# Block sums of the down projection's weights made by accumulating DMAs in DRAM, ten tiles in seven products, six raw slots

## The reference, cut to what matters

```python
def conv_gated_ffn(h, w_up, conv_w, conv_b, w_down):
    u = h @ w_up
    up = jnp.pad(u, ((0, 0), (CONV_W - 1, 0), (0, 0)))
    c = conv_b + sum(up[:, j:j + S] * conv_w[j] for j in range(CONV_W))
    gate, val = c[..., :D_FF], c[..., D_FF:]
    return (jax.nn.silu(gate) * val) @ w_down
...
    x = x + mixed @ w_o[l]
    h = rms_norm(x, norm_ffn[l])
    x = x + conv_gated_ffn(h, w_up[l], conv_w[l], conv_b[l], w_down[l])
return rms_norm(x, norm_final)
```

## Time and profile before

| | |
|---|---|
| time, median of 3 runs | 1064.83 us (1064.59 to 1065.46) |
| profiled execution | 1064.66 us, its span 1062.9 us |
| PE busy, share of the span | 1053.1 us, 99% |
| DVE | 803.6 us, 76% |
| ACT | 614.6 us, 58% |
| POOL | 9.6 us, 1% |
| moved by DMA | 201.65 MB, mean 190 GB/s |
| PE's granted clock | 0.999 |

### The profile page before, as it was taken

How to read it: one execution, slowest core, us unless ns; L and a number is a source line. 1 busy time by engine, 2 the same in 40 slices (tenths; PEclk the granted TensorE clock), 3 DMA queues, 4 the chain that set the end, 5 groups by cost and what they waited for, 6 DMA issues and landing times.

```text
span 1062.9 us, 17535 instructions
## 1 busy us (share of the span) xinstructions
PE 1053.1 (99%) x5963; PEld 908.0 (85%) x5963; DVE 803.6 (76%) x1193; ACT 614.6 (58%) x946; POOL 9.6 (1%) x30
## 2 busy tenths in 40 slices
PE   9999999999999999999999999999999999999997
PEld 8888888888888888888888888888888888888885
DVE  5677677776555787777877778777777989988886
ACT  6956475746455655555555555555555655545553
POOL 1000000000000000000000000000000000000000
PEclk9999999999999999999999999999999999999999
DMA  9575656554556566655666556665566666665663
GB/s 295 175 236 160 182 172 178 161 177 139 184 173 194 167 203 190 194 179 180 201 193 194 180 178 199 195 194 181 175 201 195 212 200 204 199 218 177 216 207 129
DMA packets 171330, 201.65 MB, mean 190 GB/s; under 512 B 8580, under 2 KB 138340, under 8 KB 171168
## 3 DMA queue, kind: packets, MB, share of 16 engines
q1 hardware_dynamic: 170576, 199.59, 60.1%
q0 software_dynamic: 400, 1.27, 0.4%
q10 hardware_dynamic: 320, 0.34, 0.1%
HBM read 199.06 MB, written 2.11 MB: 189 GB/s over the span
## 4 chain that ended last, share of the span: by engine, by line
PE 98%; DMA 1%; DVE 0%; SPq 0%; ACT 0%; issue 0%; DVEq 0%
PE tr_ps L1507 15%; PE pj L1507 15%; PE pj L1259 9%; PE pj L1509 8%; PE tr_ps L1509 8%; PE pj L1247 5%; PE pj L1248 5%; PE pj L1249 5%; PE pj L1261 5%; PE sc_ps L1247 5%; PE sc_ps L1248 5%; PE sc_ps L1249 5%; PE pj L1274 3%; PE pj L1276 1%; PE tr_ps L1248 1%; PE tr_ps L1247 1%
## 5 line engine op out<-in xcount | busy, mean ns | idle before, releaser
L798 DVE TENSOR_TENSOR split<-raw,split 128x1024 fp32r<-128x1024 f32 x282 | 340.9, 1223 | 146.4 <-ACT split L486 140.8
L486 ACT ACTIVATE split<-raw 128x1024 fp32r<-128x1024 f32 x276 | 287.6, 1057 | 105.5 <-PE pj L1509 33.0
L1507 PE MATMUL tr_ps<-act_split,split 128*128 128x512 f32 x704 | 245.5, 392 | 0.0
L1507 PE MATMUL pj<-act_split,split 128*128 128x512 f32 x704 | 245.0, 391 | 0.0
L1509 PE MATMUL pj<-act_split,split 128*128 128x256 f32 x704 | 197.1, 280 | 0.0
L1509 PE MATMUL tr_ps<-act_split,split 128*128 128x256 f32 x704 | 197.1, 280 | 0.0
L1507 PEld LDWEIGHTS pj<-act_split,split 128*128 128x128 f32 x704 | 131.6, 187 | 28.9
L1507 PEld LDWEIGHTS tr_ps<-act_split,split 128*128 128x128 f32 x704 | 131.7, 187 | 28.8
L1259 PE MATMUL pj<-act_split,split 128*128 128x512 f32 x416 | 147.8, 399 | 0.0
L1509 PEld LDWEIGHTS tr_ps<-act_split,split 128*128 128x128 f32 x704 | 133.1, 189 | 0.0
L1509 PEld LDWEIGHTS pj<-act_split,split 128*128 128x128 f32 x704 | 133.1, 189 | 0.0
(11 more groups left out here) (244 smaller groups left out, 1498.1 us busy)
## 6 DMA issues: line engine op xcount, KB each, us to landing
raw<-w_up SPq DMA_DIRECT2D x176, 512.0 KB, 4.3
raw<-w_down SPq DMA_DIRECT2D x88, 512.0 KB, 4.4
raw<-w_in SPq DMA_DIRECT2D x72, 512.0 KB, 3.8
raw<-w_o SPq DMA_DIRECT2D x32, 512.0 KB, 4.3
nat<-x SPq DMA_DIRECT2D x8, 256.0 KB, 6.6
key_bias<-nft_dram SPq DMA_DIRECT2D x4, 512.0 KB, 5.1
result<-nat SPq DMA_DIRECT2D x7, 256.0 KB, 3.1
gfin<-norm_final POOLq DMA_DIRECT2D x1, 1024.0 KB, 5.0
```

What stands on the lines that cost most here:

```text
L486: act.activation(hi[:, slot, 0:TILE], raw[:, slot, 0:TILE], ACT.Copy).then_inc(hi_done, 1)
L798: dve.tensor_tensor(lo[:, slot, 0:n], raw[:, slot, 0:n], hi[:, slot, 0:n].bitcast(F32), ALU.subtract).then_inc(lo_done, 1)
L1507: pe.matmul(up_banks[v][b].rearrange("p (a n) -> p a n", a=2), wh[:, c, b * P:(b + 1) * P], act_split[:, :, k, :], start=k == 0, stop=Fals ...
```

## The change

Ten tiles, kt 4 to 13, are done in seven products instead of seven tiles, and SUMS_AFTER sets them closer together. The sums of weight blocks are no longer added by DVE: from the third tile of w_o until 24 tiles before the end of the up projection Pool issues, for each of the 20 pairs of kt and group, two copies of 512 KB from w_down into two new DRAM tensors (t13_dram, t42_dram) and then accumulating DMAs of 256 KB within DRAM: T1 and T3, then T2 onto W22, then T4 onto W21. Six DMAs a sum, spread over four rounds, each step paced by PE's tile count (pace) and waiting for the DMAs of the round before; tsum_s counts finished sums. In the down projection SP loads all parts: part 0 whole, part 1 its half (W22, 256 KB), parts 2 and 3 from the DRAM sums. Two more slots, raw_4 and raw_5, stand where t13 and t24 stood, so loads go up to six tiles ahead. The order of the products in parts 2 and 3 changes with the layout of t42_dram. S1 is kept in the place of A21 in g_hi and g_lo, the other three in s_hi and s_lo with 384 columns. The buffers whole and sums of combine become two sets. combine takes four tiles instead of five. The squares and gains of the first two column blocks move from the start of group 1 to behind its last sums tile, and gfin is loaded once group 0 is combined.

```diff
-SUM_KT = (2, 4, 6, 8, 10, 12, 14)
+SUM_KT = tuple(range(4, 14))
 PLAIN_KT = tuple(kt for kt in range(DOWN_TILES) if kt not in SUM_KT)
-SUMS_AFTER = ((5, 9, 12, 15, 18, 22, 25), (5, 8, 11, 14, 16, 19, 21))
+SUMS_AFTER = ((5, 6, 7, 8, 11, 12, 14, 15, 18, 19), (4, 5, 6, 7, 9, 10, 12, 13, 14, 15))
+EXTRA = 2
+COMBINE = {0: (0,), 1: (1, 2), 2: (3,), 3: (4,)}
 A11, A21, A12, A22 = (0, 0), (0, 1), (1, 0), (1, 1)
-S3, S1, S2, S4 = range(4)
+S2, S4, S3, S1 = range(4)
...
-def loaded(d):
-
-    return d[1] == "plain" or d[2] < 2
-
-
 def sums_index(t):
 
     return sum(1 for d in DOWN[:t] if d[1] == "sums" and d[2] == 0)
 
 
-LOADS = [t for t, d in enumerate(DOWN) if loaded(d)]
-
-
 def raw_slot(t):
 
-    return LOADS.index(t) % RING
+    return t % RING if t < 2 * RING else (t - RING) % (RING + EXTRA)
+
+
+def raw_before(t):
+
+    return [s for s in range(t) if raw_slot(s) == raw_slot(t)]
 
 
 def slot_loads(t):
 
-    return T_DOWN // RING * 16 + (32 if raw_slot(t) % 2 == 0 else 0) + 16 * (LOADS.index(t) // RING + 1)
+    slot = raw_slot(t)
+    return (T_DOWN // RING * 16 + (32 if slot % 2 == 0 else 0) if slot < RING else 0) + 16 * (len(raw_before(t)) + 1)
+
+
+TSUMS = 2 * len(SUM_KT)
+TSUM_LAGS = 5
+TSUM_FIRST, TSUM_LAST = T_WO + 2, T_DOWN - 24
...
-        t13 = sb("t13", [P, TILE])
+        raw_4 = sb("raw_4", [P, TILE])
         assert sbuf.cursor <= top
+        sbuf.cursor = region_end
+        duo_0 = sb("duo_0", [P, MT, 512])
         sbuf.cursor = top
-        t24 = sb("t24", [P, TILE])
+        raw_5 = sb("raw_5", [P, TILE])
         assert sbuf.cursor <= nc.sbuf_usable_end
         sbuf.cursor = act_at
-        s_hi = sb("s_hi", [P, len(SUM_KT), 512], R32)
-        s_lo = sb("s_lo", [P, len(SUM_KT), 512], R32)
-        duo = sb("duo", [P, MT, 512])
-        whole, sums = duo[:, 0], duo[:, 1]
+        s_hi = sb("s_hi", [P, len(SUM_KT), 384], R32)
+        s_lo = sb("s_lo", [P, len(SUM_KT), 384], R32)
         assert sbuf.cursor <= act_end
         sbuf.cursor = act_at
         z_gain = sb("z_gain", [P, MT, 512])
+        duo_1 = sb("duo_1", [P, MT, 512])
+        wholes, sums_of = (duo_0[:, 0], duo_1[:, 0]), (duo_0[:, 1], duo_1[:, 1])
+        whole, sums = wholes[0], sums_of[0]
...
-        d_w = [sem(f"d_w{i}") for i in range(RING)]
+        d_w = [sem(f"d_w{i}") for i in range(RING + EXTRA)]
+        t_copy, t_first, t_second, t_third = [[sem(f"{n}{i}") for i in range(2)] for n in (
+            "t_copy", "t_first", "t_second", "t_third")]
+        tsum_s = sem("tsum_s")
...
+        t13_dram = nc.dram_tensor("t13_dram", (TSUMS, P, TILE), F32).ap()
+        t42_dram = nc.dram_tensor("t42_dram", (TSUMS, P, TILE), F32).ap()
...
-        def down_source(t):
-
-            if loaded(DOWN[t]):
-                return raw[:, raw_slot(t)]
-            return t13 if DOWN[t][2] == 2 else t24
+        def down_raw(t):
+
+            return raw[:, raw_slot(t)] if raw_slot(t) < RING else (raw_4, raw_5)[raw_slot(t) - RING]
...
-            for i, t in enumerate(LOADS):
-                g, kind, part, kt = DOWN[t]
-                sp.wait_ge(lo_done, T_DOWN + (LOADS[i - RING] + 1 if i >= RING else i - (RING - 1)))
-                sp.dma_start(wide(raw, raw_slot(t)),
-                             wdn[kt][:, :, (2 * g + part) * 512:(2 * g + part + 1) * 512]).then_inc(d_w[raw_slot(t)], 16)
+            for t, (g, kind, part, kt) in enumerate(DOWN):
+                if t < RING:
+                    sp.wait_ge(lo_done, T_DOWN + t - (RING - 1))
+                elif raw_before(t):
+                    sp.wait_ge(lo_done, T_DOWN + raw_before(t)[-1] + 1)
+                else:
+                    sp.wait_ge(glo_s, UP_STEPS)
+                dst = down_raw(t)[:, 0:TILE]
+                if kind == "plain" or part == 0:
+                    sp.dma_start(dst.rearrange("p (c n) -> p c n", c=2),
+                                 wdn[kt][:, :, (2 * g + part) * 512:(2 * g + part + 1) * 512]).then_inc(d_w[raw_slot(t)], 16)
+                elif part == 1:
+                    sp.dma_start(dst[:, 512:TILE], wdn[kt][:, 1, (2 * g + 1) * 512:(2 * g + 2) * 512]).then_inc(d_w[raw_slot(t)], 16)
+                else:
+                    j = sums_index(t - part)
+                    sp.wait_ge(tsum_s, j + 1)
+                    sp.dma_start(dst, (t13_dram, t42_dram)[part - 2][j]).then_inc(d_w[raw_slot(t)], 16)
...
-            pool.wait_ge(glo_s, UP_STEPS)
+            def weights(j):
+
+                return wdn[SUM_KT[j % len(SUM_KT)]], slice(j // len(SUM_KT) * 1024, j // len(SUM_KT) * 1024 + 512), \
+                    slice(j // len(SUM_KT) * 1024 + 512, j // len(SUM_KT) * 1024 + 1024)
+
+            steps = (TSUMS + TSUM_LAGS - 1) * 4
+
+            def pace(i, k):
+
+                pool.wait_ge(mm_done, TSUM_FIRST + (4 * i + k) * (TSUM_LAST - TSUM_FIRST) // steps)
+
+            for i in range(TSUMS + TSUM_LAGS - 1):
+                if i < TSUMS:
+                    pace(i, 0)
+                    w, left, right = weights(i)
+                    pool.dma_start(t13_dram[i], w[:, 0, left.start:right.stop]).then_inc(t_copy[i % 2], 16)
+                    pool.dma_start(t42_dram[i], w[:, 1, left.start:right.stop]).then_inc(t_copy[i % 2], 16)
+                j = i - 1
+                if 0 <= j < TSUMS:
+                    pace(i, 1)
+                    w, left, right = weights(j)
+                    pool.wait_ge(t_copy[j % 2], 32 * (j // 2 + 1))
+                    pool.dma_start(t13_dram[j, :, 0:512], w[:, 0, right], accum_op=ALU.add).then_inc(t_first[j % 2], 16)
+                    pool.dma_start(t13_dram[j, :, 512:TILE], w[:, 1, right], accum_op=ALU.add).then_inc(t_first[j % 2], 16)
+                j = i - 2
+                if 0 <= j < TSUMS:
+                    pace(i, 2)
+                    pool.wait_ge(t_first[j % 2], 32 * (j // 2 + 1))
+                    pool.dma_start(t42_dram[j, :, 512:TILE], t13_dram[j, :, 0:512], accum_op=ALU.add).then_inc(t_second[j % 2], 16)
+                j = i - 3
+                if 0 <= j < TSUMS:
+                    pace(i, 3)
+                    pool.wait_ge(t_second[j % 2], 16 * (j // 2 + 1))
+                    pool.dma_start(t42_dram[j, :, 0:512], t42_dram[j, :, 512:TILE], accum_op=ALU.add).then_inc(t_third[j % 2], 16)
+                j = i - 4
+                if 0 <= j < TSUMS:
+                    pool.wait_ge(t_third[j % 2], 16 * (j // 2 + 1))
+                    if j > 0:
+                        pool.wait_ge(tsum_s, j)
+                    pool.memset(small[:, 94:95], 0.0).then_inc(tsum_s, 1)
+
+            pool.wait_ge(z_s, 8)
             pool.dma_start(gfin[:], norm_final.partition_broadcast(P)).then_inc(d_gf, 16)
...
-                if loaded(DOWN[t]):
-                    act.wait_ge(d_w[raw_slot(t)], slot_loads(t))
-                else:
-                    act.wait_ge(sum_s, 4 * sums_index(t - part) + 2 * part - 2)
+                act.wait_ge(d_w[raw_slot(t)], slot_loads(t))
                 act.wait_ge(mm_done, T_DOWN + t - (RING - 1))
-                act.activation(hi[:, slot, c0:TILE], down_source(t)[:, c0:TILE], ACT.Copy).then_inc(hi_done, 1)
+                act.activation(hi[:, slot, c0:TILE], down_raw(t)[:, c0:TILE], ACT.Copy).then_inc(hi_done, 1)
 
             def sums_hi(q):
 
                 act.wait_ge(s_fp, 4 * q + 4)
-                act.activation(s_hi[:, q], sums[:], ACT.Copy).then_inc(shi_s, 1)
+                act.activation(s_hi[:, q], sums[:, 0:384], ACT.Copy)
+                act.activation(g_hi[:, 2 * SUM_KT[q], P:2 * P], sums[:, 384:512], ACT.Copy).then_inc(shi_s, 1)
...
                     if t == SUMS_END[g]:
                         act.wait_ge(mm_done, T_DOWN + SUMS_END[g])
-                        act.wait_ge(slo_s, len(SUM_KT))
-                        if g == 1:
-                            act.wait_ge(comb_s, 8)
-                            act.wait_ge(z_s, 6)
-                            act.wait_ge(zsq_s, 2)
-                        act.activation(sums[:], p1, ACT.Copy).then_inc(first_s, 1)
-                if t == GROUP_END[0]:
-                    act.wait_ge(comb_s, 8)
-                    act.wait_ge(z_s, 6)
+                        if g == 0:
+                            act.wait_ge(slo_s, len(SUM_KT))
+                        act.activation(sums_of[g], p1, ACT.Copy).then_inc(first_s, 1)
+                if t == SUMS_END[1]:
                     squares(0)
-                if t == GROUP_END[0] + 3:
+                if t == SUMS_END[1] + 1:
                     squares(1)
                 if t == SUMS_END[1] + 3:
...
-                dve.tensor_tensor(sums[:, 0:2 * P].rearrange("p (a n) -> p a n", a=2),
+                dve.tensor_tensor(sums[:, 2 * P:4 * P].rearrange("p (a n) -> p a n", a=2),
                                   whole[:, 0:2 * P].rearrange("p (a n) -> p a n", a=2),
                                   whole[:].rearrange("p (b m n) -> p b m n", b=2, m=2)[:, :, 1], ALU.subtract).then_inc(s_fp, 1)
```

(45 more changed lines are left out.)

12 lines of the change are left out of this document (8 added, 4 removed).

## The result

The changed kernel takes 1070.31 us (median of 12 runs, 1067.6 to 1078.8) against 1064.71 us of the kernel before on the same chip (12 runs, 1063.7 to 1066.3): a ratio of 1.0059, 95% interval 1.0039 to 1.0079. It is slower, by more than the 0.2% that can be told from no change; forecast were 1061.1 us.

A forecast was written before the change was run, and what follows sets the result against it. PE was taken to bound the kernel. 1064.66 us less 4.08 for 18 fewer matmuls plus 0.3 for DVE's bunching gave 1060.9, on the median 1061.1 us; own range 1060.4 to 1062.5, whole range 1060.3 to 1082.

The forecast's parts named there:

- What bounds the kernel: Whole kernel: PE is 98% of the chain of waits, and the down projection costs its matmuls and nothing else.
- PE's saving: Down projection: 18 matmuls fewer at 0.2265 us each, 4.08 us saved, all on the path.
- cheap end: Background sums, w_o and up projection: 6.8 us of engine time a round at 310 GB/s, within 8.2 us free; no cost.
- dear end: Background sums: accumulates move each byte twice, 10.2 us a round, 23.0 us needed in 21.0; 40 us over 20 rounds.
- The rival: w_o and up projection: background traffic fills the DMA engines, w_up loads fall behind, PE waits; 1075 us, chance 0.22.
- The cover of 5.7 us: Up projection: 5.7 us of load delay stay hidden, while a step's two copies take 3.4 us; free.
- DVE in the down projection: DVE loses work in total, but needs 7.53 us in a 7.47 us period of group 0; 0.3 us charged.
- the bunching: Group 0: sums tiles one plain tile apart, 0.3 us on DVE (0 to 1); loads there need 328 GB/s.
- Pool's issues beside DVE: Pool's issue of 120 DMAs slows no DVE instruction running beside it; nothing charged.
- Loads in the down projection: Larger sums tiles need 274 GB/s, 328 in the bunched run, against 346 seen; 0 us charged, between 0 and 12.
- The tail: End of down projection: two moved gains, 2.4 us, fit DVE's idle gaps; 0 us, 1 us as upper bound.
- What would show it: Signs of a wrong forecast: PE waits on DVE's splits, ACT on raw<-w_up, w_up landing far above 4.3 us.

The follow-up runs named there:

- no_traffic: Changed kernel without the background DMAs, parts 2 and 3 of sums tiles loaded straight from w_down; 1062.68 us, ratio 0.9970 to the kernel before.
- six_again: The kernel six_steps, unchanged, run a second time; 1063.77 us, ratio 1.0000 to the kernel before.
- after: The changed kernel itself, with its four paced steps per round, in its first set of runs; 1070.31 us, ratio 1.0059 to the kernel before.
- no_accumulate: Changed kernel with all 120 background DMAs, but the four of 256 KB per sum overwrite instead of add; 1064.0 us, ratio 0.9998 to the kernel before.
- after_again: The changed kernel, unchanged, run a second time; 1071.61 us, ratio 1.0066 to the kernel before.
- six_steps: Changed kernel with the six DMAs of a sum in six paced steps instead of four; 1070.02 us, ratio 1.0026 to the kernel before.
- even: Changed kernel with the sums tiles spread more evenly among the plain tiles (other SUMS_AFTER); 1080.06 us, ratio 1.0127 to the kernel before.
- mixed_no_traffic: Changed kernel without background DMAs, add_values one tile earlier only for sums tiles after a single plain tile; 1062.63 us, ratio 0.9975 to the kernel before.

## Why the prediction was wrong

**What bounds the kernel, PE's saving:** right. no_traffic shows the edit without its price, at a ratio of 0.9970 where 3.8 us are 0.9964.

**Background traffic, cheap end:** this is the step that failed, the value taken "with little trust" because the software queue's row was nearest. The 6.8 us that it put on a round measured 9.7. That row held plain small loads; it says nothing of accumulates. The dear end, 10.2 us a round with each accumulated byte moved twice, was right: 9.7 us measured. Both ends charged 20 rounds in the up projection; by the pacing four of them start in w_o, where the share before was 0.54 (240 to 345 us), so the dear end was priced too high as well.

**What the dear end costs:** by the prediction's arithmetic (9.7 + 12.8 us in 21.0) it would be 30 us. It was 8.1 and 6.2 us of stalls in the two profiled executions of after, and none in six_again. The 0.61 of the earlier trace rows isn't a fixed need: beside the background traffic the loads of w_up take less engine time per byte. The table of queues from 345 to 585 us, before and then six_again:

```profile
q1 hardware_dynamic: 45650, 45.33, 61.1%
```

```profile
q1 hardware_dynamic: 45167, 44.85, 56.3%
q0 software_dynamic: 9783, 23.59, 44.3%
```

That is 3.23 us of engine time per MB and then 3.01 (3.06 in after, 3.04 in no_accumulate). The sum just fits. The rival's mechanism was the right one, its place too; its time of 1075 was 5 us too high.

**The cover of 5.7 us:** the reading was that two copies delay a load by 3.4 us. The loads of after land up to 8 us late. Its table of queues from 423 to 440 us, ahead of the first stall:

```profile
q1 hardware_dynamic: 2842, 2.82, 49.2%
q0 software_dynamic: 729, 1.85, 48.9%
```

The loads get half of the engines and 2.82 MB / 17 us = 166 GB/s where they need 189. What counts is the whole queue of background transfers that is out together, not one pair. The Trainium skill, DMA: Bandwidth & Descriptors, section Queues, rings and completion order, says that an engine round-robins between the queue rows it has work for, packet by packet. The even halves of this row agree with it; no run here shows the turns themselves.

**What follows a stall:** not in the sum at all. The lower clock added 1.5 us behind each of two of the three stalls of after and behind one of three in after_again, and the slower pitch 7.6 us in the one and next to nothing in the other.

**DVE in the down projection:** the size was off. 0.3 us for the bunching, up to 1; it was 1.6. The bunched run, which I feared, costs little; the place of add_values in DVE's order costs 0.8 us a time. The prediction counted DVE's work per period, not which split waited behind it.

**Pool's issues beside DVE:** nothing charged, nothing found. A full split of DVE in the up projection takes 1223 ns before and after, and no_accumulate, with all 120 issues, loses 1.4 us there. **Loads in the down projection:** 0 us charged; 1.1 us in no_traffic, at most 0.4 in after (at 878 us, with a load of 6.9 us in its chain), none in wide_placed.

**The tail:** right. DVE's last half starts at 1069.57, with 1.09 us of idle time ahead of it where the earlier trace rows has 2.02; from the last matmul to the end it is 7.9 us in both.

**What would show it:** the signs named for the wrong case (PE on splits, ACT on raw<-w_up, landing far above 4.3) are what the trace shows, with two that were not named, the clock behind a stall and the pitch.

What stays open: why PE falls into the slower pitch and out of it. In the up projection it changed only at a break in PE's stream, but not at each, and six_steps and even began with it. The kernels without background traffic (no_traffic, mixed_no_traffic, all runs of before) never took over 2.2 us more than their median; their profiled runs have it in the attention stage alone, where it costs little. That their other runs have no more of it is not shown. Nor is it known why the granted clock fell behind some of the longer stalls and not behind others. Nor is it known why even, with four runs, has a median 10 us above that of after: its profiled run is 3.8 us longer, of which the down projection is 3.0.

## What to carry to other kernels

Cost an accumulating DMA from DRAM to DRAM at twice its bytes, and check it against the free engine time of the fullest stretch, not of the whole window. Spread the background transfers one at a time and leave about a tenth of the engines free: what hurts is a queue of them that delays a load past its cover. A stall of TensorE so caused can cost twice its length where the granted clock falls behind it, and can leave a slower pitch for hundreds of us. If a kernel's runs scatter by several us while its waits don't explain it, compare the lengths of like steps before trusting one profiled execution.

## What was not expected of the hardware

- TensorE has two pitches for the same stream of matmuls of 512 and 256 columns, 0.347 and 0.353 us a pair, both at a granted clock of 1.00; 11.09 or 11.31 us a step, 2%. In the up projection either held until PE's stream was broken for 0.2 us or more (fifteen changes in seven profiled runs; six_steps and even began with the slower). The slower one is found without any background traffic, too.
- Accumulates from DRAM to DRAM: 173 GB/s of engine time by destination; plain copies in the same places 287 to 308.
- Engine time of loads per MB falls from 3.23 us to 3.01 to 3.06 when a second queue is busy, so shares of different runs don't add.
- Behind a wait of PE of 1.8 us, its granted clock was 0.61 over the next 4 us; behind one of 2.2 us in even it stayed at 1.00.
- Pool's issue took 0.54 us for a plain DMA between DRAM tensors and 0.81 to 0.84 us for an accumulating one, 1.15 for the second of two in a row (0.56 for the plain one in the earlier trace rows).
